# Modulation products on GpSimd in operations of 1024 words, new shares per stage, one-column sums spread over other work

## The chip, the cores and the metric

The kernel runs on one core of a Trainium2 chip. The metric is the time of one execution in device microseconds (us). Of the kernel before there are three timed runs, 3175.03, 3181.24 and 3182.52, with a median of 3181.24, and one profiled execution.

## What is computed

The reference is a stack of two models in float32 on 256 tokens of width 1024. The first block has two layers of feed-forward, mixer, feed-forward. The second takes its output and runs two layers, the first also on 256 context tokens, in which every normalization is shifted and scaled, and every residual gated, by vectors made from a condition:

```python
def adaln(cond, w, b):
    m = jax.nn.silu(cond) @ w + b
    return m.reshape(m.shape[:-1] + (N_MOD, D_MODEL))

def ffn_sublayer(h, m, g, w13, w2, base):
    hn = modulate(rms_norm(h, g), m[:, :, base], m[:, :, base + 1])
    return h + 0.5 * m[:, :, base + 2] * swiglu_2(hn, w13, w2)
```

`w` is 1024 x 9216 per layer; there is one condition for the latent tokens and one for the context. The change concerns the product `silu(cond) @ w`, a row vector times a matrix, which the kernel calls the modulation.

## The kernel before

The work is a list of phases (norm, ffn, dense, index, softmax, stick, conv, final and others), and every engine runs through the same list with its own instructions. Weights stream from HBM in units of 2048 words per partition through a ring of three buffers. ScalarE rounds a unit to a high part (L417), VectorE subtracts it to get the low part (the lo-split, L430), and TensorE multiplies each tile three times, high by high, low by high and high by low (`mm`, L742). SyncE issues the loads.

There are nine feed-forward stages. I call the first eight f0 to f7: f0 and f1 are layer 0 of the first block, f2 and f3 its layer 1, f4 and f5 the first feed-forward of the second block on X and on the context C, f6 the second one of that layer, f7 the first of the next. Each stage is a loop of 11 groups of 256 hidden columns (`step`), which uses three units a step and raises `s_used` for each.

**The modulation.** Because this product needs each of 18.9 million weights once, for one or two rows, GpSimd makes it beside the feed-forward stages. The matrix is cut in units of 256 output columns, 36 per layer, 72 in all (`MOD = 256`). A unit that serves both conditions (the first 20 of layer 0) has two states, the others have one. `modulate` runs in the stages f0 to f7, on a list of units per stage (`mods`, given by a table of first and last units). A unit's weights come in two halves of 1024 words per partition, loaded by GpSimd's own queue (`mod_load`, L660). For each half and state GpSimd scales four blocks of 256 words by a column of the condition (L679), adds the blocks by 512 words (L682) and by 256 words into an accumulator (L684, L686, L687). A sum over the eight chunks of the contraction is thus made within each partition; what is left is a sum over the 128 partitions. When a unit is complete `s_made` is raised (L689) by the number of its states.

Before a unit GpSimd waits on `s_used`, so that its units are paced along the stage. The last thing TensorE does in such a stage is to wait for `s_made` to reach the stage's total (`made_by[f]`).

**The sums over partitions.** TensorE makes them as matmuls with one column of ones (`mod_sums`), two per accumulator, 184 in all, each in two records of the trace. Their results lie in PSUM until VectorE adds the bias and puts them in `modc` (`mod_add`). They are made in six lots (`shares`): f0's in the index phase of layer 0, f1's and f2's in that of layer 1, f3's in the final phase of the first block, f4's and f5's at the end of their own stage, f6's and f7's at the start of the convolution. In the index phases TensorE also works on `pieces` of the gate projection between the attention's steps (`beside.go`).

The final phase of the first block also waits for two loads that GpSimd issues when its work for f3 is over: the last gain and the context C.

In f5 GpSimd issues, four at a time before each of the first eight units, 32 small DMAs that build bias tiles for the attention (`bias_tiles`, L703).

Of the kernel before, what the change touches and what calls it, by code (L numbers as in the profile page):

```python
# [105 lines left out]
def program(nc, t, out):  # L106
    with ExitStack() as ctx:
# [100 lines left out]
        def vcols(name, k):  # L208
# [6 lines left out]
        slots = {**{f: [flat[:, MOD * i:MOD * (i + 1)] for i in range(24)] for f in range(4)},  # L215
                 4: [flatPJ[:, at:at + MOD] for at in (*range(0, 2048, MOD), *range(NPJ, NPJ + 2048, MOD))],
                 6: [flatPJ[:, MOD * i:MOD * (i + 1)] for i in range(8)],
                 7: [flatPJ[:, MOD * i:MOD * (i + 1)] for i in range(8, 16)]}
        slots[2], slots[5] = slots[2][12:], slots[4]
# [3 lines left out]
        def modulation(l, first, last, at):  # L223

            out, at = [], iter(at)
            for m in range(first, last):
                n_s = 2 if l == 0 and m * MOD < 5 * D else 1
                out.append((l, m, [next(at) for _ in range(n_s)]))
            return out

        mods = [modulation(l, first, last, slots[f]) for f, (l, first, last) in enumerate(
            ((0, 0, 10), (0, 10, 16), (0, 16, 24), (0, 24, 36), (1, 0, 10), (1, 10, 20), (1, 20, 28), (1, 28, 36)))]
# [412 lines left out]
        def _(pool):  # L645
# [7 lines left out]
            halves = [0]  # L653
# [8 lines left out]
            def modulate(ph, at, beside):  # L662

                part = ph["mods"]
                for i in range(2):
                    mod_load(part, i, at)
                for i in range(2 * len(part)):
                    _, m, accs = part[i // 2]
                    if i % 2 == 0:
                        pool.wait_ge(s_used, ph["u0"] + 3 * (10 * (i // 2) // len(part)) + 2)  # L670
                        beside(i // 2)
                    halves[0] += 1
                    pool.wait_ge(s_mod[i % 2], 16 * ((halves[0] + 1) // 2))
                    for st, acc in reversed(list(enumerate(accs))):
                        w = mod_raw[at][i % 2]
                        o = w if st == 0 else mod_product
                        for c in range(4):
                            k = 4 * (i % 2) + c
                            p = nc.gpsimd.tensor_scalar(o[:, MOD * c:MOD * (c + 1)], w[:, MOD * c:MOD * (c + 1)],  # L679
                                                        cond[:, k, st:st + 1], None, ALU.mult)  # L680
                        link(p)
                        link(nc.gpsimd.tensor_tensor(o[:, 0:2 * MOD], o[:, 0:2 * MOD], o[:, 2 * MOD:4 * MOD], ALU.add))  # L682
                        if i % 2 == 0:
# [4 lines left out]
                    if i % 2:  # L688
                        pool.sem_inc(s_made, len(accs))  # L689
                    if i + 2 < 2 * len(part):  # L690
                        mod_load(part, i + 2, at)
# [14 lines left out]
            for n, ph in enumerate(phases):  # L706
# [19 lines left out]
                elif ph["kind"] == "ffn" and ph["mods"]:  # L726
# [3 lines left out]
                    modulate(ph, int(ph["f"] >= 4), bias_tiles if ph["x"] is C else lambda h: None)  # L730
# [7 lines left out]
        def _(pe):  # L738
# [34 lines left out]
            def mod_sums(share, bank):  # L773
# [4 lines left out]
                at = 0  # L778
                for _, m, accs in parts:
                    for k in range(MOD // P):  # L780
                        for acc in accs:
                            i = mm(ps[:, bank, at:at + 1], acc[:, k * P:(k + 1) * P], cc("ones"))
                            at += 1
                i.then_inc(sem("mods_summed"), 1)
                summed.append(1)
# [126 lines left out]
            def ffn(ph, nx, nb):  # L912
# [91 lines left out]
                if ph["sums"]:  # L1004
                    mod_sums(ph["sums"], 3)
# [7 lines left out]
            for n, ph in enumerate(phases):  # L1013
# [8 lines left out]
                if kind == "norm":  # L1022
                    plain = ph["shift"] is None
                    for b in range(1 if follows(n - 1) and plain else 0, NB if plain else 1):
                        norm_turn(ph, b)
                elif kind == "turn":
# [24 lines left out]
                elif kind == "index":  # L1051
# [7 lines left out]
                    beside.go(sum(PACE["index"]))  # L1059
# [3 lines left out]
                    mod_sums(ph["sums"], 5)  # L1063
# [62 lines left out]
                elif kind == "final":  # L1126
                    if ph.get("sums"):
                        mod_sums(ph["sums"], 3)
                elif kind == "conv":
                    mod_sums(ph["sums"], 4)  # L1130
                    for k in range(DC):
# [8 lines left out]
                        i.then_inc(sem("conv_turned"), 1)  # L1140
                    for _ in range(4):
# [245 lines left out]
        def _(dve):  # L1387
# [87 lines left out]
            def mod_add(share, bank):  # L1475
# [3 lines left out]
                for n_s, parts in itertools.groupby(share[1], lambda x: len(x[2])):  # L1479
                    parts = list(parts)  # L1480
                    l, nk = parts[0][0], len(parts) * (MOD // P)
# [398 lines left out]
```

## Time and profile before

| | |
|---|---|
| median of three runs | 3181.24 us |
| profiled execution | 3180.6 us |
| its span, first to last instruction | 3178.7 us |
| TensorE matmuls busy | 2657.7 us, 84% |
| VectorE busy | 1431.8 us, 45% |
| ScalarE busy | 1172.4 us, 37% |
| GpSimd busy | 1778.6 us, 56% |
| mean granted clock of TensorE | 0.891 of 2.4 GHz |
| moved by DMA | 496.11 MB, 156 GB/s |

A busy share is an average over stages that have different limits. What a stage waits for is read from its own rows: where an engine sat idle, how long, and what released it. In the rows PE is TensorE, DVE is VectorE, ACT is ScalarE and POOL is GpSimd; a name with a q behind it is the engine's queue, that is an instruction which does no work but sets a semaphore.

### The profile page before, as it was taken

What the parts mean: (1) busy time and instruction counts of PE and PEld (TensorE: products, weight loads), DVE (VectorE), ACT (ScalarE), POOL (GpSimd) and SP (SyncE); (2) the same over time, 40 slices, a digit from 0 to 9 for tenths busy, and PEclk for the clock granted to TensorE, in tenths of its full rate; (3) what the DMA queues carried; (4) which work ended last, traced back from release to release, by engine and by line L of the source; (5) the groups of instructions that cost most, each with busy time, mean ns of one, the idle gap of its engine ahead of it and who ended that gap; (6) DMA issues with size and microseconds to landing.
All of it is one profiled execution on the core that took longest, in us unless ns stands there. A gap on an engine that the chain in (4) does not pass through costs nothing.

```text
span 3178.7 us, 33443 instructions
## 1 busy us (share of the span) xinstructions
PE 2657.7 (84%) x11901; PEld 2163.6 (68%) x11901; DVE 1431.8 (45%) x1617; ACT 1172.4 (37%) x1354; POOL 1778.6 (56%) x1425
## 2 busy tenths in 40 slices
PE   7960389889959858989974995995899999999898
PEld 6850377678748747667863884884667887877787
DVE  4530143565525523455542553552424555554554
ACT  4420233544324323444432442442413444344443
POOL 5999611039979961104995995995000997960000
PEclk9985689899979978989996996996957999998999
DMA  7641232256636632235762773993402776754453
GB/s 234 212 155 40 69 100 80 93 179 211 199 111 214 206 102 92 74 113 188 233 213 80 237 235 92 239 257 84 161 1 67 230 232 200 235 180 151 139 185 119
DMA packets 312488, 496.11 MB, mean 156 GB/s; under 512 B 14478, under 2 KB 221610, under 8 KB 312266
## 3 DMA queue, kind: packets, MB, share of 16 engines
q1 hardware_dynamic: 289306, 412.48, 39.8%
q0 software_dynamic: 22800, 81.35, 9.0%
q8 instruction: 57, 0.93, 0.1%
q10 hardware_dynamic: 288, 1.05, 0.1%
q14 instruction: 37, 0.30, 0.0%
HBM read 493.77 MB, written 1.05 MB: 156 GB/s over the span
## 4 chain that ended last, share of the span: by engine, by line
PE 46%; POOL 42%; DVE 4%; issue 3%; ACT 3%; DMA 1%; ACTq 0%; DVEq 0%; SPq 0%; POOLq 0%; PEldq 0%
PE ps L742 42%; POOL arena L679 23%; POOL arena L682 8%; POOL arena L686 3%; POOL arena L684 3%; POOL arena L660 3%; PE ps L816 2%; POOL arena L687 2%; PE ps L823 1%; POOL arena L703 1%; ACT whi L417 1%; DVE wlo L430 0%; PE ps L937 0%; PE ps L908 0%; DVE arena L1524 0%
## 5 line engine op out<-in xcount | busy, mean ns | idle before, releaser
L430 DVE TENSOR_TENSOR wlo<-raw,whi 128x2048 fp32r<-128x2048 f32 (+5 forms) x405 | 923.4, 2282 | 600.7 <-ACT whi L417 598.8
L742 PE MATMUL ps<-whi,HThi 128*128 128x512 f32 (+2 forms) x2360 | 954.9, 405 | 67.2 <-ACT arena L1188 20.3
L679 POOL TENSOR_SCALAR arena<-arena,cond 128x256 f32<-128x256 f32 x736 | 902.1, 1238 | 91.8 <-PE ps L742 77.6
L742 PE MATMUL ps<-wlo,HThi 128*128 128x512 f32 (+2 forms) x2360 | 931.4, 395 | 0.0
L742 PE MATMUL ps<-whi,HTlo 128*128 128x512 f32 (+2 forms) x2360 | 931.2, 395 | 0.0
L417 ACT ACTIVATE whi<-raw 128x2048 fp32r<-128x2048 f32 (+4 forms) x405 | 753.1, 1861 | 443.3 <-PE ps L742 426.5
L742 PEld LDWEIGHTS ps<-whi,HThi 128*128 128x128 f32 x2360 | 453.1, 192 | 171.1 <-issue 27.1
L742 PEld LDWEIGHTS ps<-wlo,HThi 128*128 128x128 f32 x2360 | 452.2, 192 | 96.4
L742 PEld LDWEIGHTS ps<-whi,HTlo 128*128 128x128 f32 x2360 | 453.8, 192 | 86.1
L660 POOL DMA_DIRECT2D arena<-in_mod_w_dram x144 | 116.1, 806 | 464.5 <-DVEq L350 393.4
L682 POOL TENSOR_TENSOR arena<-arena 128x512 f32<-128x512 f32 x184 | 318.1, 1729 | 15.4
L742 PE MATMUL ps<-whi,AThi 128*128 128x512 f32 x792 | 310.0, 391 | 1.1
L742 PE MATMUL ps<-wlo,AThi 128*128 128x512 f32 x792 | 308.6, 390 | 0.0
L742 PE MATMUL ps<-whi,ATlo 128*128 128x512 f32 x792 | 308.2, 389 | 0.0
L713 POOL TENSOR_TENSOR wlo<-raw,whi 128x896 fp32r<-128x896 f32 x36 | 87.9, 2441 | 360.7 <-ACT whi L417 360.7
L908 PE MATMUL ps<-cst,X 128*128 128x128 f32 x96 | 16.6, 333 | 242.1 <-POOLq L689 240.4
L908 PEld LDWEIGHTS ps<-cst,X 128*128 128x128 f32 x96 | 13.8, 173 | 245.7 <-issue 241.7
L742 PE MATMUL ps<-cst,arena 128*128 128x1 f32 x368 | 73.2, 335 | 126.3 <-POOLq L689 121.9
L742 PEld LDWEIGHTS ps<-whi,AThi 128*128 128x128 f32 x792 | 148.7, 188 | 34.9 <-issue 4.7
L742 PEld LDWEIGHTS ps<-wlo,AThi 128*128 128x128 f32 x792 | 148.7, 188 | 31.1
L742 PEld LDWEIGHTS ps<-whi,ATlo 128*128 128x128 f32 x792 | 148.7, 188 | 30.1
L1262 ACT ACTIVATE AThi<-ps 128x512 fp32r<-128x512 f32 x99 | 59.1, 597 | 290.1 <-PE ps L937 290.1
(192 smaller groups left out, 2098.0 us busy)
## 6 DMA issues: line engine op xcount, KB each, us to landing
raw<-in_ffn_w_dram SPq DMA_DIRECT2D x330, 512.0 KB, 4.6
raw<-in_w_ffn_gu_dram SPq DMA_DIRECT2D x176, 512.0 KB, 4.7
arena<-in_mod_w_dram POOLq DMA_DIRECT2D x144, 512.0 KB, 4.6
raw<-in_w_ffn_down_dram SPq DMA_DIRECT2D x88, 512.0 KB, 4.3
raw<-in_w_in_dram SPq DMA_DIRECT2D x40, 1024.0 KB, 5.1
raw<-in_even_w_in_dram SPq DMA_DIRECT2D x12, 1024.0 KB, 5.0
raw<-in_conv_w_in_dram SPq DMA_DIRECT2D x12, 1024.0 KB, 5.1
raw<-in_w_out_dram SPq DMA_DIRECT2D x8, 1024.0 KB, 5.0
```

What stands on the lines that cost most here:

```text
L417: i = nc.scalar.activation(whi[0:rows, r, a:b], raw[0:rows, r, a:b], ACT.Copy)
L430: i = nc.vector.tensor_tensor(wlo[0:rows, r, a:b], raw[0:rows, r, a:b], whi[0:rows, r, a:b].bitcast(F32), ALU.subtract)
L660: pool.dma_start(dst, kn(t["mod_w_2"][l], 4 * (i % 2), 4, m * MOD, MOD)).then_inc(s_mod[i % 2], 16)
L679: p = nc.gpsimd.tensor_scalar(o[:, MOD * c:MOD * (c + 1)], w[:, MOD * c:MOD * (c + 1)], cond[:, k, st:st + 1], None, ALU.mult)
L682: link(nc.gpsimd.tensor_tensor(o[:, 0:2 * MOD], o[:, 0:2 * MOD], o[:, 2 * MOD:4 * MOD], ALU.add))
L684: link(nc.gpsimd.tensor_tensor(acc, o[:, 0:MOD], o[:, MOD:2 * MOD], ALU.add))
L686: link(nc.gpsimd.tensor_tensor(acc, acc, o[:, 0:MOD], ALU.add))
L687: link(nc.gpsimd.tensor_tensor(acc, acc, o[:, MOD:2 * MOD], ALU.add))
L713: nc.gpsimd.tensor_tensor(wlo[at], raw[at], whi[at].bitcast(F32), ALU.subtract).then_inc(s_lo_pool, 1)
L742: return nc.tensor.matmul(o, lhsT, rhs, start=first, stop=last)
L816: i = nc.tensor.matmul(S[:, o:o + ow], lh, rh, start=False, stop=j == len(mine) - 1)
L1262: A(AT[own][0][:], ps[:, 2, :].rearrange("p (c t) -> p c t", c=2), ACT.Copy).then_inc(sem("ffn_act_hi"), 1)
```

## The change

GpSimd's `modulate` now works on whole halves. One product multiplies 1024 words by four columns of the condition, each repeated over 256 words (`broadcast_to`), into a buffer of its own, for each half. Then 2048 words are folded to 1024, 512 and 256 by three additions, for each state once. The loads of the next unit are issued behind the product that reads the buffer last. `s_made` is raised by the last addition of each state, and GpSimd waits for it.

The table of units per stage changes from (0: 0 to 10), (0: 10 to 16), (0: 16 to 24), (0: 24 to 36), (1: 0 to 10), (1: 10 to 20), (1: 20 to 28), (1: 28 to 36) to the one in the diff, where f4 has units of both layers; the accumulators (`slots`) move accordingly.

On TensorE `mod_sums` becomes `sums_of`, which collects the columns, and `sum_columns(n)`, which makes the next n. In the index phases two columns follow each of the 18 pieces, ahead of the transposes that the sums followed before. At the ends of f4 and f5, 13 columns are made, the others behind the matmuls of the next norm. In the final phase 16, the rest in the next norm. In the convolution four follow each of its eight passes. VectorE's `mod_add` for f3 moves from the final phase to the norm behind it.

```diff
-        mod_product = flatPJ[:, 2048:3072]
+        mod_product = [flatPJ[:, 2048:4096], flatPJ[:, NPJ:NPJ + 2048]]
...
         mods = [modulation(spans, slots[f]) for f, spans in enumerate(
+            ([(0, 0, 7)], [(0, 7, 14)], [(0, 14, 20)], [(0, 20, 32)], [(0, 32, 36), (1, 0, 9)], [(1, 9, 20)], [(1, 20, 28)], [(1, 28, 36)]))]
...
-                    for st, acc in reversed(list(enumerate(accs))):
-                        w = mod_raw[at][i % 2]
-                        o = w if st == 0 else mod_product
-                        for c in range(4):
-                            k = 4 * (i % 2) + c
-                            p = nc.gpsimd.tensor_scalar(o[:, MOD * c:MOD * (c + 1)], w[:, MOD * c:MOD * (c + 1)],
-                                                        cond[:, k, st:st + 1], None, ALU.mult)
-                        link(p)
-                        link(nc.gpsimd.tensor_tensor(o[:, 0:2 * MOD], o[:, 0:2 * MOD], o[:, 2 * MOD:4 * MOD], ALU.add))
-                        if i % 2 == 0:
-                            link(nc.gpsimd.tensor_tensor(acc, o[:, 0:MOD], o[:, MOD:2 * MOD], ALU.add))
-                        else:
-                            link(nc.gpsimd.tensor_tensor(acc, acc, o[:, 0:MOD], ALU.add))
-                            link(nc.gpsimd.tensor_tensor(acc, acc, o[:, MOD:2 * MOD], ALU.add))
...
+                    for st, acc in enumerate(accs):
+                        for half in range(2):
+                            if st == 0:
+                                pool.wait_ge(s_mod[half], 16 * units_before[0])
+                            by = cond[:, 4 * half:4 * half + 4, st:st + 1].broadcast_to([P, 4, MOD])
+                            p = nc.gpsimd.tensor_tensor(mod_product[at][:, 1024 * half:1024 * half + 1024].rearrange("p (c n) -> p c n", c=4),
+                                                        mod_raw[at][half].rearrange("p (c n) -> p c n", c=4), by, ALU.mult)
+                            if st == len(accs) - 1 and i + 1 < len(part):
+                                link(p)
+                                mod_load(part, 2 * i + 2 + half, at)
+                            elif half:
+                                link(p)
+                        q = mod_product[at]
+                        for n in (4 * MOD, 2 * MOD):
+                            link(nc.gpsimd.tensor_tensor(q[:, 0:n], q[:, 0:n], q[:, n:2 * n], ALU.add))
+                        p = nc.gpsimd.tensor_tensor(acc, q[:, 0:MOD], q[:, MOD:2 * MOD], ALU.add)
+                        p.then_inc(s_made, 1)
+                        pool.wait_ge(s_made, acc_made[0] + 1)
+                        acc_made[0] += 1
...
+            def sum_columns(n=None):
+
+                for o, acc in columns[:n]:
+                    i = mm(o, acc, cc("ones"))
+                if columns and (n is None or n >= len(columns)):
+                    i.then_inc(sem("mods_summed"), 1)
+                    summed.append(1)
+                del columns[:n]
...
-                    mod_sums(ph["sums"], 3)
+                    sums_of(ph["sums"], 3)
+                    sum_columns(13)
...
-                    beside.go(sum(PACE["index"]))
+                    sums_of(ph["sums"], 5)
+                    for _ in range(sum(PACE["index"])):
+                        beside.go(1)
+                        sum_columns(2)
+                    sum_columns()
...
-                    mod_sums(ph["sums"], 5)
```

## Rows read from the trace of the kernel before

**Rows 1.** The page, part 4: shares of the chain by engine

```profile
PE 46%; POOL 42%; DVE 4%; issue 3%; ACT 3%; DMA 1%; ACTq 0%; DVEq 0%; SPq 0%; POOLq 0%; PEldq 0%
```

**Rows 2.** Timeline of PE, ends of f0 to f5: start, length, what [idle before]

```profile
364.99 1.97 PE L908 MATMUL ps<-cst,X 128*128 128x128 f32 x8 [155.67 <-POOLq L689]
...
909.63 1.97 PE L908 MATMUL ps<-cst,X 128*128 128x128 f32 x8 [40.64 <-POOLq L689]
...
1148.04 1.97 PE L908 MATMUL ps<-cst,X 128*128 128x128 f32 x8 [44.11 <-POOLq L689]
...
1707.37 0.37 PE L742 MATMUL ps<-cst,arena 128*128 128x1 f32 x1 [54.32 <-POOLq L689]
...
1948.59 0.34 PE L742 MATMUL ps<-cst,arena 128*128 128x1 f32 x1 [31.19 <-POOLq L689]
...
2192.59 0.34 PE L742 MATMUL ps<-cst,arena 128*128 128x1 f32 x1 [36.40 <-POOLq L689]
```

**Rows 3.** Windows, one step in f4: us, PE, PEld, DVE, ACT, POOL busy (instructions)

```profile
1776.66:1793.45 16.79, 16.79 (x77) 13.91 (x76) 9.08 (x6) 6.78 (x6) 15.55 (x13) 1.00 0.67 219
```

**Rows 4.** Windows, f4 and f5 to PE's end; last: clock, DMA share, GB/s

```profile
1740.08:1917.40 177.32, 176.05 (x804) 145.60 (x804) 95.18 (x66) 74.32 (x68) 165.98 (x119) 1.00 0.70 231
1979.02:2156.19 177.17, 176.09 (x804) 145.61 (x804) 96.63 (x66) 74.56 (x68) 166.74 (x146) 1.00 0.95 237
```

**Rows 5.** Timeline of GpSimd: loads one unit apart, beside PE and alone

```profile
76.22 0.81 POOL L660 DMA_DIRECT2D arena<-in_mod_w_dram  x1 [0.59 <-POOL arena L687]
...
115.93 0.81 POOL L660 DMA_DIRECT2D arena<-in_mod_w_dram  x1 [0.60 <-POOL arena L687]
...
242.02 0.81 POOL L660 DMA_DIRECT2D arena<-in_mod_w_dram  x1 [0.30 <-POOL arena L684]
...
269.46 0.81 POOL L660 DMA_DIRECT2D arena<-in_mod_w_dram  x1 [0.30 <-POOL arena L684]
...
1679.00 0.81 POOL L660 DMA_DIRECT2D arena<-in_mod_w_dram  x1 [0.59 <-POOL arena L687]
...
1693.93 0.81 POOL L660 DMA_DIRECT2D arena<-in_mod_w_dram  x1 [0.59 <-POOL arena L687]
```

**Rows 6.** Timeline of VectorE in f0: two lo-splits

```profile
98.49 2.66 DVE L430 TENSOR_TENSOR wlo<-raw,whi 128x2048 fp32r<-128x2048 f32 x1 [1.29 <-ACT whi L417]
...
104.13 2.29 DVE L430 TENSOR_TENSOR wlo<-raw,whi 128x2048 fp32r<-128x2048 f32 x1 [1.11 <-ACT whi L417]
```

**Rows 7.** Groups of GpSimd: the bias tiles; busy us, mean ns | idle before

```profile
L703 POOL DMA_DIRECT2D arena<-in_na_rpb_dram x32 | 19.7, 622 | 20.2 <-PE ps L742 19.9 <-issue 0.3
```

**Rows 8.** Timeline of GpSimd alone, one half and one state

```profile
242.87 3.62 POOL L679 TENSOR_SCALAR arena<-arena,cond 128x256 f32<-128x256 f32 x4
246.58 1.26 POOL L682 TENSOR_TENSOR arena<-arena 128x512 f32<-128x512 f32 x1
247.92 0.72 POOL L686 TENSOR_TENSOR arena<-arena 128x256 f32<-128x256 f32 x1
```

**Rows 9.** Timeline of GpSimd, its lo-split of 896 words

```profile
488.87 2.08 POOL L713 TENSOR_TENSOR wlo<-raw,whi 128x896 fp32r<-128x896 f32 x1 [30.63 <-ACT whi L417]
```

**Rows 10.** Timeline of PE, norm ahead of f4 and first matmul of f4

```profile
1719.78 3.55 PE L742 MATMUL ps<-work,X 128*128 128x128 f32 x16 [2.02 <-DVE work L1510]
1725.39 0.50 PE L742 MATMUL ps<-whi,HThi 128*128 128x512 f32 x1 [2.06 <-DVE HTlo L1530]
```

**Rows 11.** Groups of PE: sums of f3, sums of the convolution

```profile
L742 PE MATMUL ps<-cst,arena 128*128 128x1 f32 x48 | 10.4, 352 | 54.3 <-POOLq L689 54.3
...
L742 PE MATMUL ps<-cst,arena 128*128 128x1 f32 x64 | 11.7, 319 | 1.5 <-ACTq L350 1.5
```

**Rows 12.** Waits of PE, index phase of layer 0: us, times, longest

```profile
PE ps L742 <- ACT arena L1190: 3.9, 2, 2.5
```

**Rows 13.** Timeline of VectorE, the last operation of the convolution

```profile
2943.11 0.17 DVE L1498 SCALAR_TENSOR_TENSOR modc<-modc,vec 128x8 f32<-128x8 f32 x1
```

**Rows 14.** Timeline of VectorE, final phase of the first block

```profile
1715.93 0.16 DVE L1564 RECIPROCAL small<-small 128x1 f32<-128x1 f32 x1 [58.88 <-DMA C<-in_ctx_dram]
```

More of the change, by code:

```diff
@@ L220, in program, with modulation @@
         mod_raw = [[flatPJ[:, 0:1024], flatPJ[:, 1024:2048]], [flat[:, 0:1024], flat[:, 3072:4096]]]
-        mod_product = flatPJ[:, 2048:3072]
-        def modulation(l, first, last, at):
+        mod_product = [flatPJ[:, 2048:4096], flatPJ[:, NPJ:NPJ + 2048]]
+        def modulation(spans, at):
             out, at = [], iter(at)
-            for m in range(first, last):
-                n_s = 2 if l == 0 and m * MOD < 5 * D else 1
-                out.append((l, m, [next(at) for _ in range(n_s)]))
-            return out
@@ L231, in program @@
-        mods = [modulation(l, first, last, slots[f]) for f, (l, first, last) in enumerate(
-            ((0, 0, 10), (0, 10, 16), (0, 16, 24), (0, 24, 36), (1, 0, 10), (1, 10, 20), (1, 20, 28), (1, 28, 36)))]
+            for l, first, last in spans:
+                for m in range(first, last):
+                    n_s = 2 if l == 0 and m * MOD < 5 * D else 1
+                    out.append((l, m, [next(at) for _ in range(n_s)]))
+            return out
+        mods = [modulation(spans, slots[f]) for f, spans in enumerate(
+            ([(0, 0, 7)], [(0, 7, 14)], [(0, 14, 20)], [(0, 20, 32)], [(0, 32, 36), (1, 0, 9)], [(1, 9, 20)], [(1, 20, 28)], [(1, 28, 36)]))]
@@ new lines, in modulate @@
+                for half in range(2):
+                    mod_load(part, half, at)
+                for i, (_, m, accs) in enumerate(part):
+                    pool.wait_ge(s_used, ph["u0"] + 3 * (10 * i // len(part)) + 2)
+                    beside(i)
+                    units_before[0] += 1
+                    for st, acc in enumerate(accs):
+                        for half in range(2):
+                            if st == 0:
[15 more added lines that the diff above has]
+                        acc_made[0] += 1
@@ L771, in settle, with sums_of @@
                     take(name)
-            def mod_sums(share, bank):
+            columns = []
+            def sums_of(share, bank):
                 settle(summed, "mods_added")
@@ L777, in mod_sums @@
                 pe.wait_ge(s_made, made)
[L778 to L785, printed above, removed]
+                accs = [acc[:, k * P:(k + 1) * P] for _, m, accs in parts for k in range(MOD // P) for acc in accs]
+                columns.extend((ps[:, bank, at:at + 1], acc) for at, acc in enumerate(accs))
+            def sum_columns(n=None):
[5 more added lines that the diff above has]
+                del columns[:n]
             def part(u, j, c, n, ev):
@@ L1556, in _ @@
                         V.tensor_scalar(half_rstd, rstd, 0.5, None, ALU.mult).then_inc(sem("rstd_ready"), 1)
[L1557 removed]
+                    elif phases[n - 1].get("sums"):
                         mod_add(phases[n - 1]["sums"], 3)
```

45 lines of the change are left out of this document (17 added, 28 removed).

## The prediction, made before the changed kernel was run

> **What bounds the kernel now.** I read the page first: the chain that ended last is 46% PE and 42% GpSimd [rows 1]. Two engines take turns, so next comes the timeline of PE, for what it waits longest for. Six waits name one releaser, GpSimd's queue at L689, where `s_made` is raised: 155.67, 40.64, 44.11, 54.32, 31.19 and 36.40 us at the ends of the feed-forward stages f0 to f5 [rows 2], 362 us together. Each row's start less its idle time is where PE had finished: 209.3, 869.0, 1103.9, 1653.1, 1917.4, 2156.2. Inside a stage PE doesn't wait for GpSimd: a step of 16.79 us is all busy [rows 3], and so is the stage, 176.05 of 177.32 us in f4 [rows 4]. So a shorter GpSimd can take these 362 us and nothing below them.
>
> **How fast GpSimd is.** Alone, when PE has finished, it takes 27.4 us from one unit's load to the next for two states (269.46 - 242.02) and 14.9 for one (1693.93 - 1679.00); beside PE two states take 39.7 (115.93 - 76.22) [rows 5]. What it loses, it loses to VectorE's lo-splits (L430), three a step: one that meets a GpSimd operation takes 2.66, the next 2.29 [rows 6], so the two engines keep each other waiting.
>
> I reckon by stage how much work, in us as if alone, GpSimd got done before PE finished: the need alone less the wait. f0: 10 x 27.4 - 155.7 = 118. f1: 6 x 27.4 - 40.6 = 124. f2: 4 x 27.4 + 4 x 14.9 - 44.1 = 125. f3: 12 x 14.9 - 54.3 = 124.5. f4: 10 x 14.9 - 31.2 = 118. f5: 10 x 14.9 + 32 bias DMAs of 0.62 (20) [rows 7] - 36.4 = 132.6. f6 and f7 (8 x 14.9 = 119) fit without a wait. I hold these capacities fixed: neither a stage's first gate nor VectorE's work changes.
>
> **Part 1: operations of 1024 words.** Removed per unit and state: eight scalings (four take 3.62), two additions of 512 and three of 256 words. Added: two products of 1024 words, then additions of 1024, 512 and 256. A two-tensor operation takes 0.72 us for 256 words, 1.26 for 512 [rows 8], 2.08 for 896 [rows 9]: 0.54 per 256 words, so 2.34 for 1024. No row shows a product whose second operand is a column repeated over 256 words. From below, 1.26: the addition of 512 words also reads 1024. From above, 3.62: the four scalings that it replaces. I take 2.34, the nearest, as it is the same operation. A state then costs 3 x 2.34 + 1.26 + 0.72 + 0.3 between them = 9.3. The two loads, now issued between the products, keep their number and add 2 x (0.81 + 0.34) [rows 5]: a one-state unit needs 11.6, a two-state unit 20.9. The new wait on `s_made` at each state's end stands for a link (0.08) and holds nothing else back.
>
> One rule speaks against the change. In the rows a scaling of 256 words (3.62 / 4 = 0.91) is dearer than a two-tensor operation (0.72). The Trainium skill has it the other way round (GPSIMD Engine Reference, Engine selection): one input is about line rate, two inputs about twice as slow. By that rule the scalings removed would be the cheap form and the products the dear one. The trace disagrees for a scaling by a column.
>
> **Part 2: the shares.** Sums of states per stage were 20, 12, 12, 12, 10, 10, 8, 8; they become 14, 14, 12, 12, 13, 11, 8, 8. Need against capacity gives the wait:
> f0: 7 x 20.9 = 146.3 over 118, waits 28, was 155.7: +127.7.
> f1: 146.3 over 124, waits 22.5, was 40.6: +18.1.
> f2: 125.4 over 125; 1.5 stay, as PE then waits for X: +42.6.
> f3: 139.2, late by 14.7. Queued behind it on GpSimd is the load of C, and the next norm starts 12.4 us after GpSimd's release (1719.78 - 1707.37) [rows 2, 10]; PE's end to the norm becomes 27.1, was 66.7: +39.6.
> f4: 150.8 over 118, waits 33, was 31.2: -1.9.
> f5: 11 x 11.6 + 20 = 147.6, waits 15, was 36.4: +21.4.
> f6, f7: 93 fits.
> Together 247.5. Beside this, load issue, which needs no turn against VectorE, becomes 2.3 of 11.6 us where it was 2.3 of 14.9. Of the 5 us and more lost in each of some 11 steps, 5% then falls on it: 3 us each in f3, f4, f5, and 2 in f0 and f1: +13.
>
> **Part 3: one-column sums.** A column is two records of 0.18 to 0.22 us [rows 11]; there are 184 as before. The index stages have 28 and 52 where they had 40 and 48: +4.5 - 1.5. Beside the pieces they fill part of two waits for ScalarE, 3.9 us per layer [rows 12], 0.75 each: +3. Elsewhere there PE is full, and moved work hides nothing. f4 and f5 put 13 and 9 of their 26 and 22 columns behind the norm's matmuls, where PE idles 2.06 [rows 10]; against 20 columns each before that is +2. In the convolution 11.7 us of sums stand ahead of a chain on VectorE that ends at 2943.3 [rows 11, 13]. Mixed, a pass is four transposes and four columns, 12 records of 0.22, 2.6 us; eight from 2916.5 end at 2937.3, with 3 us of tail at 2940: +3.5. Together 11.5. If none of it hides, 8 of these go.
>
> **Sum.** 247.5 + 13 + 11.5 = 272. The profiled execution took 3180.6 us (span 3178.7), the median is 3181.2: no difference that matters. 3180.6 - 272 = 2908.6, so 2909.
>
> **Rivals.**
> *Cheap product*, 1.26. Units need 9.4 and 16.6: f0 116, f1 116, f2 100 and f5 124 fit. f3 (113) is early; then the chain behind X rules, where VectorE was ready at 1715.93 - 58.88 = 1657.05 and the norm came 3.85 after its start [rows 10, 14], 7.9 from PE's end: +58.8. f4 (123) waits 5: +26. With f0 +154, f1 +39, f2 +42.6, f5 +35: 355, plus 11.5: 2814. For it: a repeated column need be read once. Against: no row shows such a discount. 0.20.
> *Dear product*, 3.62: the longer operation gains nothing, and the change doesn't do what it says. f0 to f5 have 152 products, each 1.28 dearer: 195 us less, 3104. For it: the only row with a column operand is the slow one. 0.13.
> *Slower than before.* The same place, past its point: every us on the product costs 152, so the 272 are gone at 2.34 + 1.79 = 4.13. If the repeated column needs a pass of its own, 2 x 2.34 = 4.68, that is 356 less, and f6, f7 (8 x 16.3 = 130 over 120) add 20: 3285. The skill's rule points this way, the two-tensor rows against it. 0.04.
> *VectorE late.* Its splits would stand behind GpSimd operations of 2.34 instead of 0.91. It is busy 9.08 of 16.79 us a step [rows 3]: 7.7 are free, so PE slows only if three delays exceed 2.6 each. If each passed on 0.5, 66 steps give 99: 3008. 0.03. The Trainium skill (SBUF — State Buffer, SBUF: two separate sides) says that whoever starts first keeps the shared port for the whole instruction; the 2.66 agrees.
> *Transfers in f5.* Its DMA share is 0.95, f4's 0.70 [rows 4]; faster units ask for tiles and weights sooner. If f5's gain stays away, 2933, inside the main case.
>
> **Numbers.** Main case 0.60 (2860 to 2970). The range may leave out 0.2: it runs from 2790, under the cheap product, to 3010, where the product costs 3.0; most of the dear case and the slower one are left out. Within 0.3% (10 us, about what a measurement of this kernel can tell from no change; the three runs scatter by 7.5) needs a product near 4.1: 0.01. Slower 0.04, faster 0.95.
>
> **What would show it.** The product's row alone: 2.34. A unit beside PE: 17 us with one state, 30 with two. PE's waits for GpSimd: 26, 20, none, C late by 12 behind f3, 30, 12. A step still 16.79. Wrong if the product is outside 2.0 to 2.9, if a unit beside PE costs clearly less than 1.45 times its time alone, or if PE's step lengthens.

## The result, and the profile after

| | before | after |
|---|---|---|
| median, runs in turns on one chip | 3181.88 us (4 runs) | 2832.62 us (4 runs, 2827.53 to 2835.23) |
| profiled span | 3178.7 us | 2829.1 us |
| mean granted clock of TensorE | 0.891 | 0.943 |

The ratio is 0.8905, with a 95% interval of 0.8886 to 0.8923. The forecast was 2909 in a range of 2790 to 3010: the sign and the range held, and 349 us were gained where 272 were forecast. But 2832.62 lies outside the main case (2860 to 2970, chance 0.60), and nearer to the 2814 of the rival *cheap product* than to 2909. The working below is about the 77 us gained beyond the forecast (78 between the two profiled spans).

The page of the changed kernel, parts 1 and 4, and the groups of VectorE's lo-split and of GpSimd's two main operations (busy us, mean ns | idle before):

```profile
PE 2634.2 (93%) x11901; PEld 2141.4 (76%) x11901; DVE 1600.5 (57%) x1619; ACT 1173.0 (41%) x1354; POOL 1329.1 (47%) x689
...
PE 60%; POOL 25%; DVE 5%; ACT 4%; DMA 3%; issue 2%; ACTq 0%; DVEq 0%; SPq 0%; POOLq 0%; PEldq 0%
...
L433 DVE TENSOR_TENSOR wlo<-raw,whi 128x2048 fp32r<-128x2048 f32 (+5 forms) x405 | 1086.6, 2686 | 529.0 <-ACT whi L420 526.7
L688 POOL TENSOR_TENSOR arena<-arena 128x1024 f32<-128x1024 f32 (+1 forms) x184 | 541.0, 2940 | 10.8
L679 POOL TENSOR_TENSOR arena<-arena,cond 128x1024 f32<-128x1024 f32 x184 | 422.4, 2302 | 174.3 <-issue 85.5
```

GpSimd's share of the chain went from 42% [rows 1] to 25%, and its busy time from 1778.6 to 1329.1 us. PE's busy time is nearly the same: what went is idleness of PE.

PE's timeline at the places of [rows 2], the ends of f0 and f1, f3 with the norm behind it, and f4:

```profile
224.42 1.97 PE L916 MATMUL ps<-cst,X 128*128 128x128 f32 x8 [14.79 <-POOL arena L689]
...
726.68 1.97 PE L916 MATMUL ps<-cst,X 128*128 128x128 f32 x8 [8.11 <-POOL arena L689]
...
1417.77 3.73 PE L745 MATMUL ps<-cst,arena 128*128 128x1 f32 x32
1428.29 3.78 PE L745 MATMUL ps<-work,X 128*128 128x128 f32 x16 [6.80 <-DVE work L1524]
...
1637.51 2.69 PE L745 MATMUL ps<-cst,arena 128*128 128x1 f32 x12 [12.80 <-POOL arena L689]
```

Six waits of 362 us are three of 35.7: 14.79, 8.11 and 12.80. At f3's end GpSimd was done first, by 3.0 us, and the norm still stands behind the load of C, which GpSimd issues when its work is over. The chain of work there (start, us, what):

```profile
1415.63 9.07 DMA C<-in_ctx_dram
...
1424.73 0.17 DVE small L1578
```

To split the gain I take the first transposition of each feed-forward stage. Those of f0, f1, f4 and f5 before:

```profile
33.84 0.33 PE L937 MATMUL ps<-cst,arena 128*128 128x128 f32 x1 [1.48 <-DVE arena L1581]
...
691.76 0.33 PE L937 MATMUL ps<-cst,arena 128*128 128x128 f32 x1 [2.81 <-DVE arena L1581]
...
1741.23 0.33 PE L937 MATMUL ps<-cst,arena 128*128 128x128 f32 x1 [1.26 <-DVE arena L1579]
...
1979.98 0.33 PE L937 MATMUL ps<-cst,arena 128*128 128x128 f32 x1 [1.26 <-DVE arena L1579]
```

The same places in the changed kernel:

```profile
34.09 0.33 PE L945 MATMUL ps<-cst,arena 128*128 128x128 f32 x1 [1.48 <-DVE arena L1593]
...
541.24 0.33 PE L945 MATMUL ps<-cst,arena 128*128 128x128 f32 x1 [2.82 <-DVE arena L1593]
...
1448.53 0.33 PE L945 MATMUL ps<-cst,arena 128*128 128x128 f32 x1 [1.26 <-DVE arena L1591]
...
1666.28 0.33 PE L945 MATMUL ps<-cst,arena 128*128 128x128 f32 x1 [1.26 <-DVE arena L1591]
```

| stretch | us before | us after | gain | gain, second profile | forecast | forecast with the measured product |
|---|---|---|---|---|---|---|
| f0 to f1 (f0's wait, index phase) | 657.9 | 507.2 | 150.8 | 154.6 | 135.7 | 148.3 |
| f1 to f2 | 235.1 | 203.4 | 31.6 | 30.2 | 20.1 | 32.7 |
| f2 to f3 (f2's wait, index phase) | 550.2 | 498.6 | 51.6 | 53.8 | 42.6 | 42.6 |
| f3 to f4 | 264.2 | 205.2 | 59.0 | 57.5 | 42.6 | 53.4 |
| f4 to f5 | 238.8 | 217.8 | 21.0 | 17.7 | 1.4 | 13.1 |
| f5 to f6 | 485.6 | 457.6 | 28.0 | 27.3 | 26.1 | 36.0 |
| f6 to f7 | 197.5 | 197.5 | 0.0 | 0.0 | 0 | 0 |
| f7 to f8 (convolution) | 328.7 | 320.8 | 7.9 | 7.9 | 3.5 | 3.5 |
| sum | | | 349.9 | 349.1 | 272.0 | 329.6 |

The second profile is that of the run `changed_again` below, the same kernel: single stretches differ by up to 4 us between the two, the sum does not.

The last column is the forecast's own working with one number changed. The view of L679 by source line gives its durations (ns, min/median/max). Where GpSimd runs longest beside an idle PE, at f0's end in the kernel with the old shares (below), its timeline shows one state:

```profile
L679 POOL TENSOR_TENSOR arena<-arena,cond x184: 1889/1909/4023, 36.0 to 2459.7; 128x1024 f32<-128x1024 f32 x184
```

```profile
272.74 3.75 POOL L679 TENSOR_TENSOR arena<-arena,cond 128x1024 f32<-128x1024 f32 x2
276.57 3.68 POOL L688 TENSOR_TENSOR arena<-arena 128x1024 f32<-128x1024 f32 x2
280.32 0.72 POOL L689 TENSOR_TENSOR arena<-arena 128x256 f32<-128x256 f32 x1
```

A product of 1024 words takes 1.89 us undisturbed, not 2.34. The addition of 1024 has exactly the price that was forecast, 2.34 (a row of it alone stands with the short products below). With 1.89, a state needs 2 x 1.89 + 2.34 + 1.26 + 0.72 + 0.3 = 8.4, a one-state unit 10.7 and a two-state unit 19.1. The 0.9 us per state, under the fixed capacities, are 12.6 + 12.6 + 10.8 + 11.7 + 9.9 = 57.6 of the 78 in f0, f1, f3, f4 and f5.

### The profile page after: what moved, and what is told of

It reads as the page before. It is cut to its first block, busy times and chain, and to the rows that moved or that the text cites. A ratio compares the mean times of both kernels' runs of the same rounds, so it can differ in the third digit from the quotient of the medians.

```text
span 2829.1 us, 32645 instructions
## 1 busy us (share of the span) xinstructions
PE 2634.2 (93%) x11901; PEld 2141.4 (76%) x11901; DVE 1600.5 (57%) x1619; ACT 1173.0 (41%) x1354; POOL 1329.1 (47%) x689
## 4 chain that ended last, share of the span: by engine, by line
PE 60%; POOL 25%; DVE 5%; ACT 4%; DMA 3%; issue 2%; ACTq 0%; DVEq 0%; SPq 0%; POOLq 0%; PEldq 0%
PE ps L745 55%; POOL arena L688 11%; POOL arena L679 9%; POOL arena L689 3%; DMA raw<-in_ffn_w_dram 2%; PE ps L824 2%; POOL arena L663 2%; DVE wlo L433 2%; ACT whi L420 1%; PE ps L831 1%; PE ps L945 1%; PE ps L762 0%; PE ps L916 0%; ACT work L1212 0%; DVE HTlo L1415 0%
## 5 line engine op out<-in xcount | busy, mean ns | idle before, releaser
L433 DVE TENSOR_TENSOR wlo<-raw,whi 128x2048 fp32r<-128x2048 f32 (+5 forms) x405 | 1086.6, 2686 | 529.0 <-ACT whi L420 526.7
L688 POOL TENSOR_TENSOR arena<-arena 128x1024 f32<-128x1024 f32 (+1 forms) x184 | 541.0, 2940 | 10.8
L679 POOL TENSOR_TENSOR arena<-arena,cond 128x1024 f32<-128x1024 f32 x184 | 422.4, 2302 | 174.3 <-issue 85.5
L745 PEld LDWEIGHTS ps<-whi,ATlo 128*128 128x128 f32 x792 | 148.7, 188 | 30.2
L689 POOL TENSOR_TENSOR arena<-arena 128x256 f32<-128x256 f32 x87 | 131.2, 1508 | 6.8
L1599 DVE TENSOR_TENSOR ATlo<-ps,AThi 128x512 fp32r<-128x512 f32 x99 | 68.1, 688 | 109.3 <-ACT AThi L1277 109.2
L1446 DVE TENSOR_REDUCE small<-ps 128x1 f32<-128x128 f32 (+2 forms) x60 | 26.8, 447 | 172.8 <-PE ps L824 97.0
```

The source lines that it names most:

```text
L433: i = nc.vector.tensor_tensor(wlo[0:rows, r, a:b], raw[0:rows, r, a:b], whi[0:rows, r, a:b].bitcast(F32), ALU.subtract)
L679: p = nc.gpsimd.tensor_tensor(mod_product[at][:, 1024 * half:1024 * half + 1024].rearrange("p (c n) -> p c n", c=4), mod_raw[at][half].rea ...
L688: link(nc.gpsimd.tensor_tensor(q[:, 0:n], q[:, 0:n], q[:, n:2 * n], ALU.add))
L689: p = nc.gpsimd.tensor_tensor(acc, q[:, 0:MOD], q[:, MOD:2 * MOD], ALU.add)
L745: return nc.tensor.matmul(o, lhsT, rhs, start=first, stop=last)
L1599: V.tensor_tensor(AT[own][1][:], ps[:, 2, :].rearrange("p (c t) -> p c t", c=2), AT[own][0][:].bitcast(F32), ALU.subtract).then_inc(sem("f ...
```

## The experiments

Ratios are against the kernel before on the same chip. It ran there at 3173.11, 3174.18 and 3176.83 us in the three sets, so the sets agree within 0.2% with one another. The changed kernel was run again in the second set. Where a median is set against the changed kernel's, 2831.9 of the second set is meant.

### What the product costs, and why

**Four scalings in its place.** All else is as in the changed kernel.

```diff
-                            p = nc.gpsimd.tensor_tensor(mod_product[at][:, 1024 * half:1024 * half + 1024].rearrange("p (c n) -> p c n", c=4),
-                                                        mod_raw[at][half].rearrange("p (c n) -> p c n", c=4), by, ALU.mult)
+                            for c in range(4):
+                                k = 4 * half + c
+                                p = nc.gpsimd.tensor_scalar(mod_product[at][:, 1024 * half + MOD * c:1024 * half + MOD * (c + 1)],
+                                                            mod_raw[at][half][:, MOD * c:MOD * (c + 1)],
+                                                            cond[:, k, st:st + 1], None, ALU.mult)
```

> Each product of 1024 words is again four scalings of 256 words by a column, into the same buffer; additions, shares and sums stay changed. Theory (price alone): a state costs 3.5 us more alone, one-state unit 14.1, two-state unit 26.0; against the fixed capacities PE waits 64, 58, 31, (f3) 45 to 58, 67, 43 us: 3085 to 3100. Rival (it is the number of operations that meets the splits): clearly above 3110.

Measured: 3078.91 us (3078.52 to 3083.98), ratio 0.9703 [0.9685, 0.9721], 6 below the band that was expected. So the one product is worth 247 of the 349 us. The other 94 by which this kernel beats the one before are the additions, the shares and the sums together; the additions were not put back by themselves. PE's waits (sum, times, longest):

```profile
PE ps L918 <- POOL arena L691: 124.3, 2, 66.4
PE ps L747 <- POOL arena L691: 98.4, 2, 52.6
...
PE ps L747 <- POOL work L691: 46.2, 1, 46.2
PE ps L918 <- POOL C L691: 31.6, 1, 31.6
```

In order they are 66.4, 57.9, 31.6, 45.8, 52.6 and 46.2. A product at 3.62 (four scalings [rows 8]) makes a one-state unit 14.2 us and a two-state unit 26.1. By the forecast's method f0 then got 7 x 26.1 - 66.4 = 116 us of work done before PE finished (118 were taken), f1 125 (124), f2 125 (125) and f3 125 (124.5), but f4 13 x 14.2 - 52.6 = 132, where 118 were taken.

**Four short products.** The same form as the change, one block of 256 words each:

```diff
+                            for c in range(4):
+                                k = 4 * half + c
+                                p = nc.gpsimd.tensor_tensor(mod_product[at][:, 1024 * half + MOD * c:1024 * half + MOD * (c + 1)],
+                                                            mod_raw[at][half][:, MOD * c:MOD * (c + 1)],
+                                                            cond[:, k, st:st + 1].broadcast_to([P, MOD]), ALU.mult)
```

> Each product as four tensor_tensor multiplications of 256 words with the column repeated. Theory (a fixed part of some 0.18 us per operation and 1.67 ns per word): four take 2.4 to 2.5 instead of 1.89, time 2885 to 2900. Rival (what made the four scalings dear is their shortness, not their form): four take 3.6, time 3079 as with the scalings.

Measured: one run of 2914.16 us, 14 above the band that was expected for the time, with products slightly below the price that was expected. The two kernels' views of that line, ns of one operation, first this one's:

```profile
L680 POOL TENSOR_TENSOR arena<-arena,cond x736: 602/612/2754, 35.2 to 2547.1; 128x256 f32<-128x256 f32 x184
```

and that of the four scalings:

```profile
L680 POOL TENSOR_SCALAR arena<-arena,cond x736: 912/918/3060, 35.5 to 2724.7; 128x256 f32<-128x256 f32 x184
```

The same multiplication of 256 words takes 0.61 us with a repeated column and 0.92 as a scaling. In a row they overlap a little. GpSimd's timeline beside an idle PE, first with short products, then with scalings:

```profile
233.26 4.60 POOL L680 TENSOR_TENSOR arena<-arena,cond 128x256 f32<-128x256 f32 x8
237.94 2.34 POOL L690 TENSOR_TENSOR arena<-arena 128x1024 f32<-128x1024 f32 x1
```

```profile
264.14 7.21 POOL L680 TENSOR_SCALAR arena<-arena,cond 128x256 f32<-128x256 f32 x8
```

Four short products take 2.3 us, four scalings 3.6 and the one long product 1.89. So of the 1.7 us saved per product, 1.3 come from the form and 0.4 from the length.

This kernel is also a test of the rest of the forecast, for with it a state costs 2 x 2.3 + 2.34 + 1.26 + 0.72 + 0.3 = 9.2, nearly the 9.3 that the forecast had. It took 2914, the forecast was 2909. But by stretches, in the order of the table, it gained 132.3, 13.8, 51.1, 40.9, 5.7, 14.8, 0.0 and 7.9 us: against the forecast that is 3, 6, 2 and 11 too little and 9, 4 and 4 more, so part of the agreement is errors that cancel.

**What makes it cheaper than an addition.** Two single runs replaced the operands and the arithmetic; each leaves out the true modulation values:

```diff
+                            p = nc.gpsimd.tensor_tensor(mod_product[at][:, 1024 * half:1024 * half + 1024],
+                                                        mod_raw[at][half], mod_raw[at][half], ALU.mult)
```

> The product takes the weights twice instead of a repeated column (it computes squares of the weights, not the modulation). Theory (reading one column over and over is what makes the product 1.89 us and not 2.36 like the addition of 1024 words): the product alone takes 2.3 to 2.4 us, and the time is near the forecast's 2909 less what the sums gained beyond it, some 2890. Rival (a multiplication into another buffer is cheaper than an addition in place, whatever it reads): 1.89 us, 2832.

```diff
-                                                        mod_raw[at][half].rearrange("p (c n) -> p c n", c=4), by, ALU.mult)
+                                                        mod_raw[at][half].rearrange("p (c n) -> p c n", c=4), by, ALU.add)
```

> The product's operation with an addition in place of the multiplication, same operands (it adds the condition to the weights). Theory (multiplying two tensors is cheaper on GpSimd than adding them): 2.3 to 2.4 us alone instead of 1.89, PE's waits grow by some 0.47 us a product against the fixed capacities: 2875 to 2890. Rival (it is the separate destination): 1.89 us, 2832.

Measured: 2834.55 and 2829.87 us. The line's durations, without the column:

```profile
L678 POOL TENSOR_TENSOR arena<-arena x184: 1887/1898/3943, 35.4 to 2460.2; 128x1024 f32<-128x1024 f32 x184
```

and with an addition for the multiplication:

```profile
L679 POOL TENSOR_TENSOR arena<-arena,cond x184: 1888/1909/3970, 35.4 to 2458.6; 128x1024 f32<-128x1024 f32 x184
```

So it isn't the arithmetic. The first run does not settle the operands, since it reads one tensor twice: in both forms only one stream of new words comes in. Nor is a destination of its own the cause, for GpSimd's lo-split of 896 words has that too, from two streams, and takes 2.08 [rows 9], that is 2.3 ns a word, like the additions' 2.34 for 1024 and unlike 1.89 (1.85 ns a word). That the discount belongs to a second operand which brings no new words fits all five rows, but a product of two different tensors was not run: it stays an inference.

### The shares

The old table of units, all else as changed:

```diff
-            ([(0, 0, 7)], [(0, 7, 14)], [(0, 14, 20)], [(0, 20, 32)], [(0, 32, 36), (1, 0, 9)], [(1, 9, 20)], [(1, 20, 28)], [(1, 28, 36)]))]
+            ([(0, 0, 10)], [(0, 10, 16)], [(0, 16, 24)], [(0, 24, 36)], [(1, 0, 10)], [(1, 10, 20)], [(1, 20, 28)], [(1, 28, 36)]))]
```

> The old table of units per stage with the new products and the new places of the sums. Theory (GpSimd gets as much done beside PE in each stage as before, 118 to 133 us as if alone, and a product costs 1.89): f0 has 10 x 19.1 = 191, so PE waits 73 us there instead of 14.8, none in f1 and f4 instead of 8.1 and 12.8, f5's steps lengthen less: 2864. Rival (longer operations lose less to VectorE's splits, so that f0 holds more): f0 waits under 60 us, total under 2850.

Measured: 2858.59 us (2852.3 to 2862.27), ratio 0.9008 [0.8992, 0.9025]. PE's timeline has the one wait for GpSimd that is left:

```profile
281.16 0.47 PE L916 MATMUL ps<-cst,X 128*128 128x128 f32 x1 [71.69 <-POOL arena L689]
```

f0 now needs 10 x 19.1 = 191, less its 118 is 73: measured 71.7. With a need changed by 57 us, the capacity of f0 stood. The shares are worth 27 us (2858.6 - 2831.9).

### The one-column sums

The sums in one lot each, at their old places:

```diff
-                    sum_columns(13)
+                    sum_columns()
...
-                    for _ in range(sum(PACE["index"])):
-                        beside.go(1)
-                        sum_columns(2)
-                    sum_columns()
+                    beside.go(sum(PACE["index"]))
...
+                    sums_of(ph["sums"], 5)
+                    sum_columns()
                     take("forget_log")
...
-                        sum_columns(16)
+                        sum_columns()
...
-                        sum_columns(4)
```

> The one-column sums stand again where they stood before, in one lot each; products and shares stay changed. Theory of the forecast (a column costs about 0.2 us twice wherever it stands, and little of it hides): some 8 us above the changed kernel's 2832, so 2840. Rival (in a lot of its own PE's granted clock falls to 0.5 and the matmuls behind it pay too, while beside the pieces a record takes 0.12): 5.5 us in the index phase of layer 0, 9.7 in that of layer 1, 7.9 in the convolution, 4 around f4 and f5, so 27 us above, 2859.

Measured: 2851.4 us (2844.13 to 2863.5), ratio 0.8991 [0.896, 0.9022]. The interval is wide, so both were run once more:

> The changed kernel once more, beside the others of this call: 2832, within 0.3%.

> The sums in one lot each, once more. Landmarks of the first run's trace (2 us in layer 0, 5 in layer 1, 4 at f4, 8 in the convolution, -2 at f3) give 17 us above the changed kernel of this call, 2849; by the forecast's sizes 8 us, by the rival with the clock 27.

Measured: the changed kernel 2831.92 us (2830.88 to 2839.97), ratio 0.8924 [0.891, 0.8937], and without part 3 2851.26 (2840.64 to 2865.38), ratio 0.8981 [0.8959, 0.9003]. The difference is 19 us, by the two intervals some 11 to 27. Of the forecast's 11.5 this run takes back 8 to 8.5, since the 3 for other numbers of columns in the index phases belong to the shares, which stay changed. By the stages' first transpositions, in the profiles of the second set, 7.4 of the difference lie in layer 0's index phase, 6.8 in layer 1's, 0.9 behind f4 and 7.9 in the convolution. In the first profiles of both kernels it was 2.2, 4.7, 4.3 and 7.8, so only the convolution's share is firm. The windows over the two lots in the index phases, of the second run without part 3 (us, busy times, granted clock, DMA share, GB/s):

```profile
311.30:320.70 9.40, 9.38 (x57) 9.40 (x57) 0.00 (x0) 1.84 (x1) 2.08 (x1) 0.66 0.02 7
1011.90:1032.30 20.40, 20.40 (x105) 20.40 (x105) 0.00 (x0) 1.82 (x1) 2.07 (x1) 0.55 0.01 3
```

In the kernel before, the lot of layer 0 and the stretch right behind it:

```profile
454.30:469.30 15.00, 15.00 (x81) 15.00 (x81) 0.00 (x0) 1.78 (x1) 2.08 (x1) 0.58 0.02 6
469.30:475.00 5.70, 5.14 (x17) 3.91 (x17) 1.03 (x5) 0.00 (x0) 0.00 (x0) 0.50 0.00 0
```

In the changed kernel, part of the same phase with the columns beside the pieces:

```profile
281.50:309.20 27.70, 24.96 (x136) 22.15 (x135) 20.32 (x63) 10.21 (x12) 3.28 (x1) 0.94 0.36 115
```

While PE makes nothing but one-column sums, its mean granted clock is between 0.55 and 0.66, that is, it drops within the lot from 2.4 to 1.2 GHz, although PE is never idle there, and the matmuls behind the lot still run at 0.50. Ahead of the lot of layer 0 in the kernel before it was 1.00 (440 to 454 us). The same columns between the pieces leave it at 0.94. At the low clock a record takes 0.19 us (20.4 / 105); behind f3, at full clock, it takes 0.12 (3.73 / 32, the row above).

Spreading does not keep the clock up everywhere. In the changed kernel's convolution the columns stand between transpositions, and it is low as in a lot:

```profile
2575.30:2593.60 18.30, 18.26 (x94) 18.17 (x92) 12.80 (x30) 9.29 (x23) 0.00 (x0) 0.52 0.02 5
```

What is gained there is the overlap: VectorE and ScalarE are busy beside the sums (12.80 and 9.29 of 18.30 us), where it was 2.24 and 0.00 of 11.70 us in that lot of the kernel before.

### The transfers in f5

```diff
-                    modulate(ph, int(ph["f"] >= 4), bias_tiles if ph["x"] is C else lambda i: None)
+                    modulate(ph, int(ph["f"] >= 4), lambda i: None)
...
-                    pe.wait_ge(sem("near_in"), 16 * 32)
```

This leaves out the 32 bias tiles of f5 and so their values in the attention.

> f5 without the 32 small DMAs that build the bias tiles (the attention then uses whatever lies there). Theory (f5's steps of 18.6 to 20.9 us come from transfers, whose share of the 16 DMA engines is 1.0 there): all steps are 16.79 again, the stage is 13 us shorter, 2819. Rival (VectorE's splits stand behind GpSimd operations of 1024 words): the steps stay above 18 us, 2832.

Measured: 2819.72 us (2819.12 to 2821.82), ratio 0.8882 [0.8869, 0.8895], 12.2 us below the changed kernel. Its window over f5:

```profile
1669.20:1836.20 167.00, 167.00 (x765) 138.62 (x766) 111.94 (x60) 68.13 (x62) 145.92 (x75) 1.00 0.78 252
```

The window runs from the stage's first transposition to its last. In the changed kernel that takes 180.0 us (181.9 in its second profile), with steps of up to 20.9 where the same ones took 16.8. Its windows over that stretch, over a step of f4 and over one of f5:

```profile
1666.28:1846.28 180.00, 171.53 (x764) 140.54 (x765) 106.80 (x60) 68.58 (x62) 154.66 (x106) 0.98 0.96 246
1517.54:1534.33 16.79, 16.79 (x78) 13.91 (x77) 11.77 (x7) 6.79 (x6) 15.84 (x9) 1.00 0.83 284
1740.00:1760.80 20.80, 17.25 (x77) 13.66 (x75) 8.82 (x6) 6.78 (x6) 19.08 (x19) 0.99 1.07 268
```

and its chain of waits inside f5 (start, us, what):

```profile
1715.97 4.67 DVE wlo L433
...
1734.58 4.27 DVE wlo L433
...
1739.60 16.15 DMA raw<-in_ffn_w_dram
...
1755.84 1.93 ACT whi L420
...
1757.79 2.30 DVE wlo L433
...
1760.84 15.75 DMA raw<-in_ffn_w_dram
```

In the step from 1740 the DMA share is 1.07 by the view's reckoning, and a load of weights takes 16 us to land, where the median over the kernel is 4.7. The stretch takes 167.0 with four scalings, 174.8 with the product but f5's old ten units, 180.0 with eleven and 167.0 without the tiles: a faster GpSimd is worth 8 us of delay and the eleventh unit 5, and only together with the tiles.

Crowded transfers alone don't do it either. The kernel with four scalings has the tiles, eleven units and a share of 0.99 over the same stretch, and loses nothing:

```profile
1880.14:2047.20 167.06, 167.06 (x765) 138.69 (x766) 88.14 (x60) 68.27 (x62) 157.44 (x126) 1.00 0.99 242
```

What differs is VectorE, and how long the slowest loads take. With scalings a lo-split of this stretch takes 2.47 us in the mean, and none of the 57 loads of weights takes over 12.0 to land. In the changed kernel it is 3.14 us, and 13 loads take longer than 12. Without the tiles the splits are as long (3.27), but the loads land in 4.7 (median), and no step grows. The chain above holds both, splits of 4.67 and 4.27 and loads of 16 us, one behind the other: SyncE issues the next load into a buffer when the lo-split that reads it is over. So slow loads and late splits cost time together; how the 13 us divide between them is not shown.

### A better table

After the change f0, f1 and f4 still wait for GpSimd, while f5 to f7 have room. Fewer units early, more late, and the accumulators of f6 summed at its own end:

```diff
-            ([(0, 0, 7)], [(0, 7, 14)], [(0, 14, 20)], [(0, 20, 32)], [(0, 32, 36), (1, 0, 9)], [(1, 9, 20)], [(1, 20, 28)], [(1, 28, 36)]))]
+            ([(0, 0, 6)], [(0, 6, 12)], [(0, 12, 19)], [(0, 19, 29)], [(0, 29, 36), (1, 0, 4)], [(1, 4, 14)], [(1, 14, 25)], [(1, 25, 36)]))]
...
-sums=shares[f] if f in (4, 5) else None
+sums=shares[f] if f in (4, 5, 6) else None
```

> Shares by the measured prices: 6, 6 and 7 two-state units in f0 to f2, one two-state and nine one-state units in f3, then 11, 10, 11, 11 one-state units in f4 to f7, with accumulators of f6 and f7 also in C, and f6's lot summed at its own end. Theory (fixed capacities, units of 19.1 and 10.7): waits 0, 0, 9, 0, 0, 0, 0, 0 instead of 15, 8, 0, 0, 13, 0, 0, 0; f5's steps still long; 2810. Rival (f6 and f7 now run over, or C's use makes GpSimd wait): PE waits there, 2825 or more.

Measured: 2793.89 us (2786.85 to 2799.71), ratio 0.8801 [0.8785, 0.8816]: 38 us below the changed kernel, and 16 below what was expected. The waits came as expected. Beyond them, in the profiles of that set, f3 to f4 is 5.1 us shorter and f4 to f5 17.2 where the wait there was 12.8. There are fewer columns of sums behind f3 and f4 (22 and 22 for 24 and 26), which is too little for all of it; the rest is open. One wait for GpSimd is left on PE's timeline, at f2's end:

```profile
899.29 0.47 PE L916 MATMUL ps<-cst,X 128*128 128x128 f32 x1 [7.86 <-POOL C L689]
```

Then half of the bias tiles were moved to f4, all else as in that kernel:

```diff
-bias_tiles if ph["x"] is C else lambda i: None
+{4: lambda i: bias_tiles(i) if i < 4 else None, 5: lambda i: bias_tiles(i + 4)}.get(ph["f"], lambda i: None)
```

> six_lots with half of the bias tiles (16 DMAs) issued in f4 and half in f5. Theory (f5 is held up by transfers alone): f4's DMA share stays under 0.9 and its steps at 16.79, f5's steps come back to 16.79, worth the 8 us by which f5's stage exceeded the others: 8 us under six_lots of this call. Rival (the tiles slow f4 as much as they free f5, or GpSimd's 10 us more in f4 make PE wait there): no gain.

> six_lots once more, beside the version with its bias tiles in two stages: 2794, within 0.3%, since nothing in it is changed.

Measured: 2785.37 us (2779.8 to 2795.24), ratio 0.8778 [0.8759, 0.8797], beside 2791.44 (2781.73 to 2798.94), ratio 0.8786 [0.8766, 0.8806]. In the profiles that stretch of f5 went from 177.6 to 167.5 us, while f4's took 167.4. The window over f4 of the kernel with the tiles in two stages, DMA share 0.87:

```profile
1422.00:1600.00 178.00, 176.48 (x807) 145.56 (x806) 121.93 (x66) 74.58 (x68) 159.64 (x91) 1.00 0.87 251
```

So the stage was mended as meant, but the medians differ by 6 us with intervals that overlap: a gain in total is not shown.

## Why the prediction was right, and where its numbers failed

- **What bounds the kernel.** Right. The six waits shrank from 362 to 36 us, and f6 to f7, which had none, gained 0.0.
- **The product, 2.34.** Mis-sized: 1.89. This is the step of the sum that failed, and 57.6 of the 78 us. I took the price of the addition as "the same operation", and it isn't. The rival *cheap product* gave as its reason that a repeated column need be read once, which fits the runs but isn't proved by them; its price of 1.26 was off by 0.63, the forecast's by 0.45. The *dear product* fell altogether. The band "outside 2.0 to 2.9" given as a sign of error was left, by 0.11. That the time still fell into the range is owed to its lower end, which was set for the rival: the main case, down to 2860, was missed by 27 us.
- **The rule on inputs.** The Trainium skill (GPSIMD Engine Reference, Engine selection) compares GpSimd with VectorE: one input at roughly line rate, two inputs about twice slower. The two-input half agrees here: an addition takes 2.3 ns a word on GpSimd, the lo-split of 2048 words 2.29 us, that is 1.1 ns a word, on VectorE. The other half does not hold for a scaling by a column: 0.92 us for 256 words, 3.6 ns a word, where the form with two tensors takes 0.61 for the same product.
- **Capacities held fixed.** Right within 2 us in f0 and f1, too low in f3 and f4. f0, with seven two-state units: 133.7 - 14.8 = 118.9 (118 taken). f1, with seven as well: 133.7 - 8.1 = 125.6 (124). f0 with the old shares: 191 - 71.7 = 119.3. With four short products, though, f0 and f1 took only 112 and 119. f4, with 13 one-state units, has 139.1 - 12.8 = 126.3 (118), and 132 with scalings: this is the 8 us by which the stretch f4 to f5 beats the last column. The term for load issue (+3 in f4) covers a part; the rest I can't explain. In f3 GpSimd, needing 128.4, ended its last addition 3.0 us before PE's last matmul of the stage: 131.4, where 124.5 was taken. The path behind it is the one that was forecast, release, load of C, norm: 13.5 us from that addition to the norm, forecast 12.4. PE's end to the norm is 10.5, forecast 27.1; 10.8 of these 16.6 us are the product's, the rest the larger capacity. In the second profile of the changed kernel C had landed 1.6 us before VectorE was ready for it.
- **A unit beside PE.** Two loads one unit apart are 28.3 us in f0, forecast 30. That is 1.48 times 19.1, forecast 1.45, so the smaller loss beside PE on which the +13 for load issue rested does not show in f0:

```profile
54.06 0.80 POOL L663 DMA_DIRECT2D arena<-in_mod_w_dram  x1 [0.30 <-POOL arena L679]
...
82.35 0.79 POOL L663 DMA_DIRECT2D arena<-in_mod_w_dram  x1 [0.30 <-POOL arena L679]
```

- **VectorE late.** Right in its cause, without effect in f4, and a part of the delay in f5. A lo-split of any length takes 2.69 us in the mean, where it took 2.28, and the longest 5.24, where it was 3.42. Over f4 VectorE is busy 119.67 us, where it was 95.18 [rows 4], and PE as long as before:

```profile
1447.40:1624.70 177.30, 176.05 (x804) 145.60 (x804) 119.67 (x66) 74.30 (x68) 166.19 (x84) 1.00 0.78 254
```

  The Trainium skill (SBUF — State Buffer, SBUF: two separate sides) says that of a GpSimd operation and a VectorE operation with two SBUF inputs, as the lo-split is, the one that comes first holds the shared port for its whole instruction. The trace agrees in this: with longer instructions on GpSimd the lo-splits take longer.
- **Transfers in f5.** The rival came true: the stage is 13 us longer (180.0 for 167.0), and these come back without the bias tiles, but the late lo-splits have a part in it (above). In the balance only 8 are missing, since GpSimd, with 13 us more, leaves no wait there (5.1 by the method).
- **The sums.** Mis-sized: 19 (11 to 27) for the 8 to 8.5 that are comparable. In the index phases the forecast held the clock fixed: I priced a column by [rows 11], which were made at a low clock, and took it for the same in a lot and between the pieces. In the convolution a mixed pass took 2.29 us where 2.6 was forecast, still at the low clock. The last operation of that chain shows it:

```profile
2595.56 0.17 DVE L1512 SCALAR_TENSOR_TENSOR modc<-modc,vec 128x8 f32<-128x8 f32 x1
```

- **What adds up.** 57.6 product, 8 in f4, 5.6 in f3, 4.4 in the convolution, 9.0 in the stretch from f2 (by the runs without part 3, 4.7 to 6.8 of it the sums), 1.4 in f0 and f1, less 8.0 in f5: 78.0. But in the second profile of the changed kernel f4's item is 4.6, f2's 11.2 and that of f0 and f1 3.8. The product's 57.6 and the convolution's 4.4 stand clear of that scatter, and f5's 8.0 does; the small ones carry little.

## What to carry to other kernels

When one engine waits at the ends of stages, reckon for each stage how much work the other gets done beside it, and charge the change against that: the method gave the waits within some 2 us in f0 and f1, with the new shares and with the old, once the price of the operation was known, and was 8 us off in f4. The weakest number was the one operation that no row showed, on which 152 copies hung; it is worth looking for what the nearest row does not share with it, here that both its operands bring new words. And when one stage has been cured, read what is near its end there before loading it further: in f5 a DMA share of 0.95 cost nothing, later lo-splits cost nothing, and both together cost 13 us. Moving units to stages with room gave 38 us more than the change had.

## What the runs showed of the hardware that was not expected

- On GpSimd 1024 words by a repeated column take 1.89 us, and as long with the weights themselves as the second operand or with an addition for the multiplication. An addition of two different streams takes 2.34. For 256 words the product takes 0.61 us, as a scaling by a column 0.92.
- TensorE's mean granted clock is 0.55 to 0.66 while it makes only one-column sums, without a pause between them, and 0.50 right behind; a record takes 0.19 us there and 0.12 at full clock. Between pieces of a projection the same columns leave it at 0.94, between transpositions of the convolution it is 0.52.
- 32 small transfers, 2.1 of 496 MB, in a stage whose DMA share is 0.78 without them raise it to 0.96, in single steps to 1.07, and the landing of a load of weights there to 16 us. A share of 0.99 over the stage, in the kernel with four scalings, delayed nothing.
